# Moving 80 VectorE dot products and their weight tiles from the delta-rule heads into the expert sum

## The reference

```python
def adaln_params(cvec, w, b):
    m = jax.nn.silu(cvec) @ w + b
    return [mi[..., None, :] for mi in jnp.split(m, ADA_CHUNKS, axis=-1)]
...
    for i in range(DEPTH):                       # DEPTH = 2
        sh1, sc1, g1, sh2, sc2, g2 = adaln_params(c, ada_w[i], ada_b[i])
        csh1, csc1, cg1, csh2, csc2, cg2 = adaln_params(c_ctx, ada_w[i], ada_b[i])
        ...
        x = x + g1 * y
        x = x + g2 * peer_ffn(modulate(x, norm2_g[i], sh2, sc2), peer_w_query[i], peer_sub_keys[i],
                              peer_u[i], peer_v[i])
        if not last:
            xc = xc + cg1 * yc
            xc = xc + cg2 * peer_ffn(modulate(xc, norm2_g[i], csh2, csc2), ...)
```

## Time and profile before

| | |
|---|---|
| median of three runs | 3681.4 us (3679.86 to 3689.94) |
| the profiled execution | 3681.4 us, span 3680.1 us |
| busy, share of the span | PE 93%, PEld 87%, DVE 76%, ACT 43%, POOL 40% |
| mean granted TensorE clock | 0.969 |
| the chain that ended last | PE 62%, DVE 18%, DMA 10%, ACT 5% |
| from HBM | 661.82 MB read, 203 GB/s over the span with the writes |

### The profile page before, as it was taken

One profiled execution on the slowest core, in us unless ns is written; L12 is line 12 of the kernel. 1 busy time (PEld: TensorE's weight loads), 2 busy tenths in 40 slices (PEclk: granted clock), 3 DMA queues, 4 the chain that ended last, 5 costly groups with the idle time before them and its releaser, 6 DMA issues.

```text
span 3680.1 us, 59883 instructions
## 1 busy us (share of the span) xinstructions
PE 3436.9 (93%) x24101; PEld 3198.8 (87%) x24101; DVE 2779.3 (76%) x4946; ACT 1600.1 (43%) x2472; POOL 1472.6 (40%) x796
## 2 busy tenths in 40 slices
PE   7997999899988999899999999999998999988899
PEld 5656999878988999889999986999998999877799
DVE  3886777648999998688888867788764777757575
ACT  2323444433334555333333336456663333457453
POOL 1334555333777777655555400586672000000000
PEclk8998999999999999999999999999999999998999
DMA  5333112423776999989999730577777888631365
GB/s 186 115 114 115 47 47 81 132 75 93 242 227 220 338 333 334 342 300 339 336 335 342 290 99 14 162 238 228 257 247 265 273 276 277 215 117 57 101 192 161
DMA packets 250819, 751.20 MB, mean 204 GB/s; under 512 B 24112, under 2 KB 101808, under 8 KB 243248
## 3 DMA queue, kind: packets, MB, share of 16 engines
q1 hardware_dynamic: 124288, 431.28, 36.4%
q10 hardware_dynamic: 89392, 181.86, 13.9%
q0 software_dynamic: 36864, 134.23, 9.6%
HBM read 661.82 MB, written 84.93 MB: 203 GB/s over the span
## 4 chain that ended last, share of the span: by engine, by line
PE 62%; DVE 18%; DMA 10%; ACT 5%; issue 3%; POOL 1%; ACTq 0%; SPq 0%; DVEq 0%
PE ps L139 60%; DMA paGg<-paG 4%; DVE paone L81 3%; DVE n_sq L114 2%; DMA ring<-in_v 2%; DVE lo L81 2%; PE ps L142 2%; ACT hi L134 2%; DMA parow<-in_u_rows,paidx 2%; DVE paR L81 2%; POOL lo L81 1%; DVE g_b L81 1%; DMA ring<-in_gdn_in 1%; ACT L130 1%; DVE g_acc L93 1%
## 5 line engine op out<-in xcount | busy, mean ns | idle before, releaser
L81 POOL TENSOR_TENSOR lo<-ring,hi 128x1024 fp32r<-128x1024 f32 x392 | 967.5, 2474 | 1046.2 <-ACT hi L134 1044.6
L134 ACT ACTIVATE hi<-ring 128x1024 fp32r<-128x1024 f32 x725 | 768.5, 1061 | 916.9 <-PE ps L139 630.3
L81 DVE TENSOR_TENSOR lo<-ring,hi 128x1024 fp32r<-128x1024 f32 (+1 forms) x333 | 406.1, 1221 | 238.1 <-ACT hi L134 237.7
L139 PE MATMUL ps<-pahh,hi 128*128 128x384 f32 (+1 forms) x1152 | 408.4, 355 | 25.3 <-POOL lo L81 22.4
L139 PE MATMUL ps<-pahl,hi 128*128 128x384 f32 (+1 forms) x1152 | 397.6, 345 | 0.0
L139 PE MATMUL ps<-pahh,lo 128*128 128x384 f32 (+1 forms) x1152 | 397.4, 345 | 0.0
L139 PE MATMUL ps<-pchh,hi 128*128 128x256 f32 x1152 | 332.8, 289 | 11.4 <-POOL lo L81 9.7
L139 PE MATMUL ps<-pchh,lo 128*128 128x256 f32 x1152 | 325.3, 282 | 0.0
L139 PE MATMUL ps<-pchl,hi 128*128 128x256 f32 x1152 | 325.0, 282 | 0.0
L139 PEld LDWEIGHTS ps<-pahh,hi 128*128 128x128 f32 x1152 | 220.8, 192 | 33.0 <-POOL lo L81 25.2
L139 PE MATMUL ps<-g_b,g_b 128*128 128x128 f32 x1856 | 233.0, 278 | 12.7 <-ACT g_b L134 9.3
(11 more groups left out here) (477 smaller groups left out, 9726.5 us busy)
## 6 DMA issues: line engine op xcount, KB each, us to landing
ring<-in_u SPq DMA_DIRECT2D x256, 512.0 KB, 4.3
ring<-in_v SPq DMA_DIRECT2D x256, 512.0 KB, 4.8
ring<-in_adat SPq DMA_DIRECT2D x80, 512.0 KB, 3.6
paA<-paga ACTq DMA_DIRECT2D x128, 192.0 KB, 4.6
paG<-paR ACTq DMA_DIRECT2D x12, 2048.0 KB, 8.7
paAg<-paA ACTq DMA_DIRECT2D x16, 1536.0 KB, 7.9
paGg<-paG ACTq DMA_DIRECT2D x16, 1536.0 KB, 22.4
ring<-in_ffn_up SPq DMA_DIRECT2D x44, 512.0 KB, 3.8
```

Of the source, the lines that this page charges most:

```text
L81: return Op(self.e.tensor_tensor(out, a, b, op) if self.real else None)
L134: return Op(self.e.activation(out, a, ACT.Copy, scale=scale) if self.real else None)
L139: return Op(self.e.matmul(out, l, r, start=start, stop=stop, skip_group_check=skip) if self.real else None)
```

## The change

`plan` no longer has the 56 late `adat` tiles. `gdn_heads` no longer calls the dots. `ada_late` gets its own memory (a row, three tiles, two halves of `n_sq` for the unused product) and returns `load` and `dot`, which `first_down` calls once per expert tile: ScalarE's queue loads `adat` tile k at i = 2k, once the dot of tile k - 3 is done, and VectorE does its one or two dots at i = 2k + 4, after that tile's row addition. The SiLU comes at i = 3, and the parameters are written at i = 118. `peer` and `peer_down` get the same calls behind a flag that stays off.

```diff
@@ plan
-    for k in range(24, 80):
-        out.append((("adat", k), d["adat"][k], 1024, True))
     add("gdn_out", 8)
@@ gdn_heads
-            rows_loaded, rows_ready, dot = ada_late(st)
-            dots_at = [{12: 2, 16: 2, 19: 2, 22: 2} for _ in range(8)]
-            dots_at[0] = {10: 1, 12: 3, 15: 3, 18: 3, 22: 2}
-            dots_at[7] = {12: 2, 16: 2, 19: 2, 22: 2, 25: 2, 28: 2, 31: 2, 33: 2, 35: 2, 37: 2}
...
-                for n in range(5):
-                    if hd == 0 and n == 0:
-                        rows_loaded()
-                    if hd == 0 and n == 3:
-                        rows_ready()
+                for _ in range(5):
                     yield True
...
-                        if engine is vector:
-                            for _ in range(dots_at[hd].get(n, 0)):
-                                dot()
...
-            dot()
             meet("gdn_heads")
@@ first_down, scalar
                 if i == 2:
                     sparse["factor"](3)
+                late[0](i)
@@ first_down, vector
                 for k in added.get(i, ()):
                     add(k)
+                late[1](i)
@@ ada_late
-        row = mem.over("late_row", [128, 3, 2, 1024], "hi")[:, 2]
-        junk = n_rs[:, :].bitcast(BF16)
+        row = alloc(st, "late_row", [128, 2, 1024])
+        tiles = [alloc(st, f"late_w{i}", [128, 1024]) for i in range(3)]
+        rest = [x.bitcast(BF16) for x in n_sq]
...
+        def load(i):
+            if i == 0:
+                act.dma(row[:, :, :], d["crow"]).then_inc(s_row, 0, 16)
+            if i == 3:
+                act.wait_ge(s_row, 0)
+                act.act(row[:, :, :], row[:, :, :], ACT.Silu).then_inc(s_silu, 0)
+            if i % 2 == 0 and i < 112:
+                k = i // 2
+                if k >= 3:
+                    act.wait_ge(s_dot, used[k - 3][-1])
+                act.dma(tiles[k % 3][:, :], d["adat"][24 + k]).then_inc(s_load[k % 3], k, 16)
+
+        def dot(i):
+            if i % 2 == 0 and 4 <= i < 116:
+                k = (i - 4) // 2
+                if k == 0:
+                    dve.wait_ge(s_silu, 0)
+                dve.wait_ge(s_load[k % 3], k)
+                for j, col in enumerate(used[k]):
+                    if col >= 2:
+                        dve.wait_ge(s_dot, col - 2)
+                    dve.dot(rest[col % 2], tiles[k % 3][:, :], row[:, j, :], dots[:, col:col + 1]).then_inc(s_dot, col)
+            if i == 118:
+                dve.wait_ge(s_dot, 79)
...
```

More of the change, by code:

```diff
@@ L1437, in peer_first @@
             first_up(name, h, A, G, R, one, ga, groups, sparse, gather, dot)
-            first_down(name, Ag, Gg, av, ga, halves, groups, sparse, gather, add)
+            first_down(name, Ag, Gg, av, ga, halves, groups, sparse, gather, add, ada_late(st))
     def sparse_rows(sparse):
@@ L1910, in first_up, with first_down @@
         vector()
-    def first_down(name, Ag, Gg, av, ga, halves, groups, sparse, gather, add):
+    def first_down(name, Ag, Gg, av, ga, halves, groups, sparse, gather, add, late):
         s_gated, s_high, s_act, s_res = S("expert_gated"), S("expert_high"), S("expert_act"), S("expert_added")
@@ L2032, in first_down, with peer @@
         rest()
-    def peer(l, a, z, name, then):
+    def peer(l, a, z, name, then, late=False):
         w = z - a
@@ L2058, in peer @@
             peer_up(l, nt, name, h, A, G, R, one, ga, groups)
-            peer_down(l, nt, name, Ag, Gg, av, halves, groups, then)
+            peer_down(l, nt, name, Ag, Gg, av, halves, groups, then, ada_late(st) if late else None)
     def peer_groups(name, A, G, Ag, Gg):
@@ L2387, in peer_up, with peer_down @@
         vector()
-    def peer_down(l, nt, name, Ag, Gg, av, halves, groups, then):
+    def peer_down(l, nt, name, Ag, Gg, av, halves, groups, then, late):
         s_act, s_res = S("expert_act"), S("expert_added")
@@ L2427, in scalar @@
                 hi_to(v[i])
+                if late:
+                    late[0](i)
                 k = i // 8
@@ L2481, in ada_late @@
     def ada_late(st):
+        s_load = [S(f"late_loaded{i}") for i in range(3)]
         s_row, s_silu, s_dot = S("late_cond_loaded"), S("late_cond"), S("late_dot")
-        row = mem.over("late_row", [128, 3, 2, 1024], "hi")[:, 2]
-        junk = n_rs[:, :].bitcast(BF16)
+        row = alloc(st, "late_row", [128, 2, 1024])
+        tiles = [alloc(st, f"late_w{i}", [128, 1024]) for i in range(3)]
+        rest = [x.bitcast(BF16) for x in n_sq]
         dots = alloc(st, "late_dots", [128, 80])
-        parts = [(k, j) for k in range(56) for j in range(2 if k < 24 else 1)]
-        left = list(enumerate(parts))
+        used, c = [], 0
         for k in range(56):
[L2490 to L2501, removed]
+            n = 2 if k < 24 else 1
+            used.append(range(c, c + n))
+            c += n
+        def load(i):
[21 more added lines that the diff above has]
+                dve.wait_ge(s_dot, 79)
                 dve.tt(mod[:, 0, 40:48, :], dots[:, 0:16].rearrange("p (m j) -> p m j", j=2),
@@ L2508, in dot @@
                 ada_scale(1, 1, "late", (0,))
[L2509 to L2519, removed]
+        return load, dot
     def swa():
```

## The result

| | before | after |
|---|---|---|
| median | 3682.89 us (3679.86 to 3689.94, 4 runs) | 3735.08 us (3724.96 to 3749.18, 4 runs) |
| profiled execution, span | 3681.4, 3680.1 | 3737.83, 3736.5 |
| TensorE's mean granted clock | 0.969 | 0.965 |

The ratio is 1.0144, 95% interval 1.0115 to 1.0172: the change makes the kernel slower by 52 us. The forecast was 3737, which is 56 us over the 3681.4 that it started from.

The account below looks back on a forecast made before the run. TensorE was taken to bound the kernel, busy nearly the whole span, with VectorE close behind in the expert sum. 3681.4 - 11 (heads) + 66.5 (expert sum) = 3737 us; range 3690 to 3775.

Parts of the forecast that it names:

- Start, 2.5: Start of the heads: without the row's load and SiLU, ScalarE begins the exponentials earlier; 1.9 to 3.2 us won, 2.5 taken.
- Head 0 alone, 4.4: Head 0, 340 to 361 us: twelve dots between the inversion's steps delay a busy VectorE; removing them wins 4.4 us.
- The middle, 0.5: Interleaved heads 1 to 7: dots hidden in VectorE's waits for TensorE; gain 0, at most 3 us, 0.5 taken.
- End, 3.4: End of the heads: last dots and parameter additions delay the last state update and copy; removing them wins 3.4 us.
- Two-dot pairs, 10.35: Expert sum, 24 tile pairs with two dots: VectorE needs 10.35 us against 8.60, adding 42 us in all.
- One-dot pairs, 9.35: Expert sum, 32 tile pairs with one dot: DMA time limits them to 9.35 us, 0.75 more each, 24 us in all.
- ScalarE, 0.5, "so ScalarE doesn't stall for it": Expert sum: 56 load issues of 0.33 us fit in ScalarE's free time; only SiLU and table load overrun, 0.5 us.
- Sum 66.5: Total time added in the expert sum: 42 + 24 + 0.5 = 66.5 us.
- The dots that fit in: Rival, expert sum: GpSimd's subtraction slips aside, pairs stay at 8.60 us, only the 11 us gain remains: 3670 us; chance 0.04.
- The gate loads that fall behind: Rival, expert sum: new tiles in the same queue delay gate loads, adding 26 us: 3763 us; chance 0.14.
- The heads gain what was said: Answers the rival that the heads gain nothing because TensorE's own order sets them: 3748 us; chance 0.09.
- TensorE's clock falls: Rival, expert sum: idle time halves TensorE's clock, two-dot pairs take at least 16.5 us: 3885 us; chance 0.02.

Follow-up runs that it names:

- experiment 5: Kernel before, its 80 dots moved to the middle of the heads (11 per head in heads 1 to 6), SiLU behind the first exponentials: 3686.58 us, ratio 1.0019.
- experiment 4: VectorE takes GpSimd's low halves of layer 0's expert tiles: in the kernel after 3725.35 us (1.0122), in the kernel before 3715.87 us (1.0111).
- dots-only kernel: Kernel after with all its dots, but the loads of all late tiles except the first three left out: 3716.36 us, ratio 1.0067.
- experiment 6: Kernel before, only 14 late tiles moved to the expert sum, 66 dots rearranged in the heads; loads after the gates 3669.10 us (0.9976), behind them 3697.70 us (1.0050).
- experiment 3: Kernel after, with the late tile load that stood just behind each group's gate loads issued just ahead of them on the same queue: 3730.94 us, ratio 1.0137.
- experiments 2 to 4: Kernel after with late tiles issued by SP (1.0209), or one load ahead of the gates (1.0137); low halves all on VectorE, kernel after (1.0122) and before (1.0111).
- the kernels with one part each: Kernel after without the dots (loads only, a column copied instead): 3724.53 us, 1.0090; without all tile loads but three (dots only): 3716.36 us, 1.0067.

## Why the prediction was right

The total was off by 2 us, the change by 3. Its sum for the expert sum was right by luck: the errors in it cancel.

- *Start, 2.5.* Measured 4.0 (330.33 to 326.36). The table load stays on the path, as in the lower of the two cases. What was missed is that the wait for the row ran 2 us longer than the one for VectorE behind it.
- *Head 0 alone, 4.4.* Measured 4.5: 8.5 at the level of 360.28 less 4.0. Levels of 5.2 came as read off head 7.
- *The middle, 0.5.* Measured -0.3 (8.5 to 8.1). The cover was real, and experiment 5 shows its edge.
- *End, 3.4.* Measured 3.6 (11.8 at the first ScalarE instruction behind the heads, less 8.1). Sum 11.8 against 11. The three instructions behind the heads scatter, though: in seven profiles with these same heads they start at 697.3 to 705.3, mean 702.3. The heads of the kernel before stand in two profiles, 712.19 and 709.54 (experiment 4), so mean against mean the gain is 8.6. The agreement within 1 us is partly luck. The clock behind the heads still falls (0.61 over the 22 us from 698), so what the upper bound allowed for that was not won.
- *Two-dot pairs, 10.35.* Measured 9.9. The mechanism was right: VectorE is full and TensorE waits for its low half. Both terms were a little large: a dot costs 1.14 start to start, not 1.26 (2 x 0.12), and GpSimd's subtraction costs the gating 2.66 - 0.48 = 2.2, not 2.4. 31 us instead of 42. The subtraction itself becomes longer (3.19 against 2.40), so part of its cost falls on GpSimd, which has time.
- *One-dot pairs, 9.35.* An undisturbed one measured 8.76: 5.43 + 1.14, 2.05 by which GpSimd's subtraction stretches a low half (2.51 to 2.54 start to start instead of 0.47), and 0.14 in which VectorE waits for ScalarE. The chain there goes round through 24 matmuls (4.41), ScalarE's two high halves (1.48) and this low half (2.6), so VectorE is not quite what bounds it. That is 5 us instead of 24. The step that failed is the DMA time that was added to each pair. Over whole groups a one-dot pair took 9.67 us, 8.9 in the dots-only kernel and about 8.66 before (groups of 34.4 to 35.1): what the loads cost stands in lumps behind the gate loads.
- *ScalarE, 0.5, "so ScalarE doesn't stall for it".* This is the step that was wrong. It looked at what the issue waits for by semaphore (a dot two tiles back) and at the 0.33 us of an issue in a quiet queue. The trace shows 7.34 us for the same instruction 3.8 to 4.5 us behind a gate load, 13 times over 2 us. The loads make up the rest of the 66: 30 us beside the 36 of the pairs, or 27 beside the dots-only kernel (673.7 less 646.8). That is 2.1 to 2.3 us per held issue, near the 2.5 of experiment 6, but not evenly: against the dots-only kernel a group is 0.8 us longer with two-dot pairs (40.7 and 39.9) and 2.9 with one-dot pairs (38.7 and 35.7). It can't all be put down to the hold itself, since the kernel of experiment 3 has one hold and the same time.
- *Sum 66.5, measured 66.0.* 36 + 30 instead of 42 + 24 + 0.5. Two terms were too large by 30 us together, and the third too small by as much.
- *Rivals.* The dots that fit in are excluded by the dots-only kernel (1.0067 against 0.9959). The gate loads that fall behind didn't show in the kernel after (1.2 us), but they do as soon as the late tiles leave that place in the queue or the pairs become faster (experiments 2 to 4): the mechanism was there, hidden by the held queue. The heads gain what was said. TensorE's clock falls in places, not in the stage (0.98); the two blocks at 0.61 and 0.76 (1863 and 2021 us) stand behind stalls.
- *What the profile would show.* Busy shares of 0.86 and 0.97 where 0.85 and 95% were named; waits put down to the low half, 72.9 us; heads' end at 700.4 where 701 was. Not so: a DMA share near 1 in the one-dot part (0.93), and VectorE has 105 us less in the heads, not 115.

The Trainium skill (SBUF — State Buffer, "Who interferes with whom") says that a VectorE instruction with two SBUF inputs and a GpSimd instruction that reads SBUF exclude each other. Experiment 4 agrees: without GpSimd's subtraction the gating takes 557 ns instead of 842 in the mean, and the longest 573 instead of 2742. The Trainium skill's figure of about 358 GB/s from HBM per core (DMA: Bandwidth & Descriptors, "Where 436 GB/s comes from") is passed here by the windows with 383 GB/s over 6 us and 400 over 8; over 260 us it was 351.

What stays open is why the issue is held. The runs show when: one tile behind a gate load on the same queue, in 13 of 13 cases in the kernel after and in 11 of 14 in experiment 6, and in none five tiles behind it; three tiles behind it only once, in experiment 3, where another late tile stood ahead of the gate loads. And they show until when: 9.6 to 12.1 us after the gate load's issue for the 12 long holds of the kernel after, 6.5 to 15.8 over all kernels. During the hold at 1650.65 the DMA share is 1.00, during the short one at 1611.11 it is 0.92. They don't show what the issue waits for, nor why three issues in the same place were not held. How the 30 us divide between the late high half, the bytes beside the gate loads and the lower clock behind a stall isn't told apart either.

## What to carry to other kernels

A DMA issued from a computing engine's queue isn't free because its semaphore is ready: look at the length of the issues themselves. Place them well after large loads with a deadline: just behind them on the same queue, just ahead of them, and on another queue all cost the same or more here; five tiles later cost next to nothing (for 14 tiles). When a stage seems to have one bound, look for transfers with a large share of its chain, even where nobody waits long for them; a faster engine only uncovers them. A total that comes out right is not yet an explanation: here only the kernels with one part each showed the second cause.

## What was not expected of the hardware

- The issue of a 512 KB load on ScalarE's queue took 0.33 us alone and, in 12 of 13 cases in the kernel after, 5.3 to 8.1 us when it came 4 us behind two loads of 1.5 MB (2.01 in the other). It ended 9.6 to 12.1 us after these, and the engine's computing stood still for up to 6.9 us.
- Over 8 us the core moved 400 GB/s at a DMA share of 1.03.
- After 3.1 us of idle time in 6, TensorE ran 24 matmuls in 7.14 us instead of 4.4. The granted clock was 0.61 in the mean of these 8 us, so mostly at the lower of its two levels (1.2 and 2.4 GHz).
- GpSimd's subtraction of 2.40 us took 3.19 us when it began beside a dot on VectorE with the gating behind it: 0.79 us more, about the 0.86 that the dot still had to run.
